# Twelve row buffers in place of eight for the expert gathers of a fused two-block transformer kernel, from set 112 on

## The chip, the cores and the metric

The kernel runs on one core of one Trainium2 chip. The metric is the device time of one execution in microseconds; the time before is the median of three runs. The profiled execution is one more execution, taken by the hardware profiler.

## The reference

Two transformer blocks run one after the other on 256 tokens of width 1024, all in float32. The first block has attention and then a layer with product-key experts; the second has a gated feed-forward network, a mixer, and another feed-forward network. The change touches the expert layer of the first block alone:

```python
def _peer(h, w_query, sub_keys, u, v):
    # 128 tokens at a time: 8 heads, 16 experts for each head, of 128 * 128 experts
    best, flat = lax.top_k(cand, PEER_TOPK)
    ...
    experts = e1 * PEER_N_KEYS + e2
    g = jax.nn.softmax(best, axis=-1)
    u_sel = jnp.take(u, experts, axis=0)
    act = jax.nn.gelu(jnp.einsum('cd,chkd->chk', xc, u_sel).astype(jnp.float32), approximate=False)
    v_sel = jnp.take(v, experts, axis=0)
    return jnp.einsum('chk,chkd->cd', (g * act).astype(v.dtype), v_sel)
```

Every token picks 8 x 16 = 128 experts. For each of them one row of `u` (1024 floats) is fetched for a dot product with the token, and one row of `v` for a weighted sum. That is 256 x 128 x 2 rows of 4 KB, 268 MB, which depend on the data and so must be gathered.

## The kernel before

The tokens stand on the 128 partitions, in two tiles `tt`. A **set** is one gathered piece: for one slot (one of the 128 experts of each token), one row for each of the 128 tokens, 128 x 1024 floats or 512 KB. There are 2 x 128 sets of `u` and as many of `v`, 512 in all, each fetched by one indirect DMA that GpSimd (POOL) issues at L745.

Slots go in groups of eight (`GB`). The list `SETS` sets the order of the gathers: u of group 0, then u of group g and v of group g-1 in turn, and v of the last group at the end. Set n is the n-th gather in this order, so sets 104 to 111 are u of group 7, sets 112 to 119 v of group 6, sets 120 to 127 u of group 8. From set 112 on there are 400 gathers, that is 25 cycles of 16 (eight of v, eight of u).

Set n lands in buffer n % 8. For n below 256 the buffers lie in `ring`, from 256 on in `arena`; it is the same eight semaphore pairs: `rows_ld[i]` counts landings, `rows_used[i]` counts uses. Before POOL issues set n it waits until set n-8 has been used (`used(pool, n - GB)`); POOL issues strictly in the order of n.

The consumers, each in the order of its own program:

- VectorE (DVE) takes every u set with one multiply-and-sum per slot (`dot_rows`, L2026). Behind the first two slots of group g it multiplies the gates of group g-1 (L2033), which ScalarE (ACT) needs for the diagonal matrices (L923).
- TensorE (PE) takes the v sets of the slots with slot % 4 != 3, six of eight (`sum_group`, L1383): a diagonal matrix of gates times the gathered rows, in two halves of 512 columns. Each half is two passes, so a slot has four MATMUL records and a group 24.
- DVE takes the other two v sets of each group (slots 3 and 7) with a multiply-add into `hx` (`add_row`, L2043).
- In some groups DVE also does part of the routing of later slots (`top_keys`, `top_pairs`, `pick`, lines 1931 to 2017), and PE and ACT compute the queries of the second tile.

Behind the last gather SyncE (SP) loads the weights of the first feed-forward network (L621) and PE begins it (L1429) once the sum is added to `hx`. The first two weight pieces are loaded earlier, once set 255 has been used and `ring` is free.

## Time and profile before

| what | value |
|---|---|
| runs (us) | 1599.96, 1591.04, 1595.07; median 1595.07 |
| profiled execution: span from first to last instruction | 1554.8 us |
| median of the runs less that span | 40.3 us |
| PE, DVE, ACT, POOL busy over the span | 79%, 67%, 27%, 37% |
| gathers from set 112 on: first issue to last issue | 384.2 to 946.3 us |

The profile gives the profiled execution's span; a time of its own beside the span isn't recorded. The 40.3 us between the median of the runs and the span stand for what lies around the first and the last instruction, and are the same for every stage. The stretch from 384.1 to 947 us holds the gathers that the change touches, and the 607.8 us behind it hold the second block.

### The profile page before, as it was taken

The page shows a single profiled execution, that of the slowest core. Times are in us where ns is not written, and L with a number is a line of the kernel's source. Part 1 is how long each engine was busy: PE and PEld are TensorE (multiplying, and loading weights), DVE is VectorE, ACT ScalarE, POOL GpSimd, SP SyncE. Part 2 cuts the span into 40 slices and gives each one's busy share as a digit, 9 for nine tenths or more (in the row PEclk, how much of TensorE's full clock was granted, in tenths as well). Part 3 has the DMA queues.
Part 4 walks back from the last instruction along what each step waited for, and adds up shares of the span by engine and source line. Part 5 has one row for each costly group of instructions (what it writes and reads, how often), then busy time and mean ns, then how long its engine had stood idle before and what let it go on. Part 6 is the DMA issues. An engine that isn't in the chain of part 4 may idle for free.

```text
span 1554.8 us, 17801 instructions
## 1 busy us (share of the span) xinstructions
PE 1233.7 (79%) x6525; PEld 893.8 (57%) x6525; DVE 1047.1 (67%) x1923; ACT 426.1 (27%) x738; POOL 572.7 (37%) x626
## 2 busy tenths in 40 slices
PE   6988896667876564575556558999999999999997
PEld 4555574234443221232222225989989999899996
DVE  5767467878588666775665564677776777656556
ACT  1145313021102100200210113333335555344332
POOL 4100016667776666767777774010010000000000
PEclk9996898779888776877787779999999999899999
DMA  9834148999999999999999999678848556355561
GB/s 329 341 121 152 34 178 309 376 363 368 389 396 377 346 379 394 379 362 388 382 368 360 390 358 344 208 269 303 288 150 297 176 168 206 128 162 190 197 207 69
DMA packets 179710, 435.47 MB, mean 280 GB/s; under 512 B 13881, under 2 KB 84610, under 8 KB 179638
## 3 DMA queue, kind: packets, MB, share of 16 engines
q0 software_dynamic: 84384, 306.26, 51.9%
q1 hardware_dynamic: 94214, 126.18, 24.3%
q10 hardware_dynamic: 1040, 2.10, 0.4%
q8 instruction: 41, 0.67, 0.2%
q14 instruction: 31, 0.25, 0.0%
HBM read 433.44 MB, written 2.14 MB: 280 GB/s over the span
## 4 chain that ended last, share of the span: by engine, by line
PE 59%; DMA 14%; POOL 11%; DVE 8%; issue 6%; ACT 2%; SPq 0%; DVEq 0%; POOLq 0%
PE quad L1429 14%; PE quad_a L1383 8%; PE quad L1383 7%; PE quad_a L1534 7%; DMA arena<-in_peer_v_dram,arena 6%; POOL arena L745 6%; PE quad_a L1443 6%; DMA ring<-in_peer_v_dram,arena 5%; POOL ring L745 5%; PE quad_a L1139 3%; PE quad_a L1235 2%; PE quad L1217 2%; PE quad_a L1611 2%; DMA ring<-in_ffn_w_gu_dram 2%; PE quad_a L1599 1%
## 5 line engine op out<-in xcount | busy, mean ns | idle before, releaser
L1383 PE MATMUL quad_a<-arena 128*128 128x512 f32 x384 | 202.2, 691 | 147.6 <-DMA arena<-in_peer_v_dram,arena 147.6
L1383 PE MATMUL quad<-ring,arena 128*128 128x512 f32 x360 | 191.1, 695 | 111.5 <-DMA ring<-in_peer_v_dram,arena 108.1
L1383 PEld LDWEIGHTS quad_a<-arena 128*128 128x128 f32 x384 | 84.6, 225 | 264.6 <-issue 264.3
L745 POOL DMA_INDIRECT ring<-in_peer_u_dram,arena x136 | 137.8, 1013 | 206.2 <-DVE arena L2006 130.8
L1383 PEld LDWEIGHTS quad<-ring,arena 128*128 128x128 f32 x360 | 79.6, 226 | 216.0 <-issue 216.0
L1429 PE MATMUL quad<-u_hi,w_hi 128*128 128x256 f32 x704 | 199.1, 283 | 2.0 <-DVE u_lo L1926 2.0
L1429 PE MATMUL quad<-u_lo,w_hi 128*128 128x256 f32 x704 | 199.1, 283 | 0.0
L1429 PE MATMUL quad<-u_hi,w_lo 128*128 128x256 f32 x704 | 198.9, 283 | 0.0
L1884 DVE TENSOR_TENSOR w_lo<-ring,w_hi 128x2048 fp32r<-128x2048 f32 x66 | 150.7, 2289 | 52.0 <-ACT w_hi L929 51.7
L697 POOL DMA_DIRECT2D arena<-in_w_ada_dram x60 | 31.8, 531 | 400.2 <-DVE arena L1677 395.3
L2026 DVE CUSTOM_DVE_ANT_0 arena<-ring,quad 128x1024 f32<-128x1024 f32 x128 | 154.7, 1220 | 35.3 <-DMA ring<-in_peer_u_dram,arena 19.1
L2026 DVE CUSTOM_DVE_ANT_0 arena<-arena,quad_a 128x1024 f32<-128x1024 f32 x120 | 144.8, 1220 | 23.7 <-DMA arena<-in_peer_u_dram,arena 18.1
L923 ACT ACTIVATE arena<-ident,arena 128x128 f32<-128x128 f32 x192 | 59.6, 389 | 355.7 <-DVE arena L2033 355.7
L745 POOL DMA_INDIRECT arena<-in_peer_u_dram,arena x120 | 130.9, 1091 | 58.7 <-PE quad_a L1383 32.3
L745 POOL DMA_INDIRECT arena<-in_peer_v_dram,arena x136 | 129.7, 954 | 43.1 <-issue 39.4
L929 ACT ACTIVATE w_hi<-ring 128x2048 fp32r<-128x2048 f32 x66 | 126.0, 1914 | 68.6 <-DMA ring<-in_ffn_w_gu_dram 68.6
L1429 PEld LDWEIGHTS quad<-u_hi,w_hi 128*128 128x128 f32 x704 | 134.6, 191 | 4.0 <-issue 1.9
L1429 PEld LDWEIGHTS quad<-u_lo,w_hi 128*128 128x128 f32 x704 | 134.4, 191 | 1.5
L1429 PEld LDWEIGHTS quad<-u_hi,w_lo 128*128 128x128 f32 x704 | 134.4, 191 | 0.0
L745 POOL DMA_INDIRECT ring<-in_peer_v_dram,arena x120 | 113.1, 943 | 40.9 <-issue 36.0
L2043 DVE SCALAR_TENSOR_TENSOR hx<-arena,hx 128x1024 f32<-128x1024 f32 x34 | 43.8, 1289 | 116.8 <-DMA arena<-in_peer_v_dram,arena 116.6
L1534 PE MATMUL quad_a<-u_hi,w_lo 128*128 128x256 f32 x288 | 81.2, 282 | 0.0
(364 smaller groups left out, 2257.2 us busy)
## 6 DMA issues: line engine op xcount, KB each, us to landing
ring<-in_ffn_w_gu_dram SPq DMA_DIRECT2D x44, 1024.0 KB, 9.3
arena<-in_w_ada_dram POOLq DMA_DIRECT2D x60, 512.0 KB, 6.4
ring<-in_ffn_w_down_dram SPq DMA_DIRECT2D x22, 1024.0 KB, 5.0
ring<-in_w_mix_in_dram SPq DMA_DIRECT2D x20, 1024.0 KB, 6.3
arena<-in_peer_w_query_dram SPq DMA_DIRECT2D x4, 2048.0 KB, 7.9
ring<-in_w_ada_dram POOLq DMA_DIRECT2D x12, 512.0 KB, 10.5
arena<-in_w_in_dram SPq DMA_DIRECT2D x3, 2048.0 KB, 35.2
arena<-in_w_out_dram SPq DMA_DIRECT2D x2, 2048.0 KB, 10.8
```

The costliest lines, as they stand in the source:

```text
L697: gp.dma_start(buffer, src).then_inc(ld_ada[i], 16)
L745: gp.indirect_dma_start(out=rows_of(n), out_offset=None, in_=t["peer_" + kind][0], in_offset=bass.IndirectOffsetOnAxis(ap=expert[tt][:, sl ...
L923: diag_ready.mark(ac.activation(diag[:, i % DIAGS], ident, ACT.Copy, scale=gate[tt][:, slot:slot + 1]))
L929: ac.activation(w_hi[slot], w_slots[slot], ACT.Copy).then_inc(hi_ready.sem, 1)
L1139: last = te.matmul(bank[0:ROWS[tt], 0:width], nT[:, k, COL0[tt]:COL0[tt] + ROWS[tt]], rhs[:, k], start=(k == 0), stop=(k == KD - 1))
L1383: last = te.matmul(sum_side[tt][:, cols], diag[:, i % DIAGS], rows_of(n)[:, cols], start=(slot == pe_slots[0]), stop=(slot == pe_slots[-1] ...
L1429: last = te.matmul(psum[c][:, w * SEQ:(w + 1) * SEQ], weight[a][:, k, (c % 2) * P:(c % 2 + 1) * P], (u_hi, u_lo)[b][:, k], start=(k == 0 a ...
L1443: last = te.matmul(psum[4 + 2 * tt + n][:, :], (h_hi, h_lo)[a][:, c, tt * P:(tt + 1) * P], weight[b][:, c % 2, n * 512:(n + 1) * 512], sta ...
L1534: last = te.matmul(bank[:, a * SEQ:(a + 1) * SEQ], w[i][:, k, cols], u[j][:, k], start=start, stop=stop)
L1884: v.tensor_tensor(w_lo[slot], w_slots[slot], w_hi[slot].bitcast(F32), ALU.subtract).then_inc(lo_ready.sem, 1)
L2026: v.tensor_tensor_reduce(out=prod[:, slot % 2], in0=rows_of(n), in1=hn_side[tt], scale=1.0, scalar=0.0, op0=ALU.mult, op1=ALU.add, accum_o ...
L2043: v.scalar_tensor_tensor(out=hx[:, tt], in0=rows_of(n), scalar=gate[tt][:, slot:slot + 1], in1=hx[:, tt], op0=ALU.mult, op1=ALU.add).then_ ...
```

## The change

From set 112 on the gathers rotate over twelve buffers in place of eight. The four more lie in `arena` at columns 0 to 4095 for sets below 256, and at 11776, 12800, 13824 and 14848 from set 256 on. Each set now knows its buffer (`buffer_of`), how many times that buffer has been used (`use_of`), and the set that had it before (`before`). All waits go by these. The first set in a new buffer waits instead for query matmuls of the second tile (`a_full`), which read what lay there. The order of the gathers, all consumers' instructions and their order stay. SP's first weight load waits for the last uses of twelve buffers instead of eight, which are uses of sets up to 255 either way.

```diff
         rows_early = [area(ring, D * i, D) for i in range(GB)]
-        rows_late = [area(arena, o, D) for o in (4096, 5120, 6144, 15872, 16896, 22024, 23048, 24072)]
+        rows_early += [area(arena, D * i, D) for i in range(4)]
+        rows_late = [area(arena, o, D) for o in (4096, 5120, 6144, 15872, 16896, 22024, 23048, 24072, 11776, 12800, 13824, 14848)]
+        BUFFERS, WIDER_AT = len(rows_early), 112
...
+        buffer_of, use_of, before = [], [], []
+        last_in = {}
+        for n in range(2 * QT * SLOTS):
+            i = n % GB if n < WIDER_AT else (n - WIDER_AT) % BUFFERS
+            buffer_of.append(i)
+            before.append(last_in.get(i))
+            use_of.append(1 if before[n] is None else use_of[before[n]] + 1)
+            last_in[i] = n
...
         def used(eng, n):
-            eng.wait_ge(rows_used[n % GB], n // GB + 1)
+            eng.wait_ge(rows_used[buffer_of[n]], use_of[n])
...
-                        for last in range(QT * SLOTS - GB, QT * SLOTS):
+                        for last in range(QT * SLOTS - BUFFERS, QT * SLOTS):
                             used(sp, last)
...
-                    if n >= GB:
-                        used(pool, n - GB)
+                    if before[n] is not None:
+                        used(pool, before[n])
+                    elif n >= WIDER_AT:
+                        pool.wait_ge(a_full.sem, a_at["pq", 1, 0] + 1)
                     elif n == 6:
                         pool.wait_ge(d_full.sem, d_at["wo", 1, 1] + 1)
+                    if n == QT * SLOTS:
+                        pool.wait_ge(a_full.sem, a_at["pq", 1, 3] + 1)
```

On POOL, around the first gather into a new buffer, the program of before reads as follows. The rows are the gathers of sets 118 to 127; `rows_used0` to `rows_used7` are the eight use counts.

```order
L745 DMA ring<-in_peer_v_dram,arena 128x1024 [waits rows_used6]
L745 DMA ring<-in_peer_v_dram,arena 128x1024 [waits rows_used7]
L745 DMA ring<-in_peer_u_dram,arena 128x1024 [waits rows_used0,routed]
L745 DMA ring<-in_peer_u_dram,arena 128x1024 [waits rows_used1]
L745 DMA ring<-in_peer_u_dram,arena 128x1024 [waits rows_used2]
L745 DMA ring<-in_peer_u_dram,arena 128x1024 [waits rows_used3]
L745 DMA ring<-in_peer_u_dram,arena 128x1024 [waits rows_used4]
L745 DMA ring<-in_peer_u_dram,arena 128x1024 [waits rows_used5]
L745 DMA ring<-in_peer_u_dram,arena 128x1024 [waits rows_used6]
L745 DMA ring<-in_peer_u_dram,arena 128x1024 [waits rows_used7]
```

The same place after the change (L760 is the line that was L745), sets 118 to 131:

```order
L760 DMA ring<-in_peer_v_dram,arena 128x1024 [waits rows_used6]
L760 DMA ring<-in_peer_v_dram,arena 128x1024 [waits rows_used7]
L760 DMA arena<-in_peer_u_dram,arena 128x1024 [waits a_full,routed]
L760 DMA arena<-in_peer_u_dram,arena 128x1024 [waits a_full] x3
L760 DMA ring<-in_peer_u_dram,arena 128x1024 [waits rows_used0]
L760 DMA ring<-in_peer_u_dram,arena 128x1024 [waits rows_used1]
L760 DMA ring<-in_peer_u_dram,arena 128x1024 [waits rows_used2]
L760 DMA ring<-in_peer_u_dram,arena 128x1024 [waits rows_used3]
L760 DMA ring<-in_peer_v_dram,arena 128x1024 [waits rows_used4]
L760 DMA ring<-in_peer_v_dram,arena 128x1024 [waits rows_used5]
L760 DMA ring<-in_peer_v_dram,arena 128x1024 [waits rows_used6]
L760 DMA ring<-in_peer_v_dram,arena 128x1024 [waits rows_used7]
```

No gather has moved. The first four of group 8 no longer wait for the v sets just ahead of them, and from there on every wait is for the set twelve earlier instead of eight.

## Rows read from the trace of the kernel before

**Rows 1.** The page: busy tenths, granted clock, DMA share and rate in 40 slices.

```profile
PE   6988896667876564575556558999999999999997
POOL 4100016667776666767777774010010000000000
PEclk9996898779888776877787779999999999899999
DMA  9834148999999999999999999678848556355561
```

**Rows 2.** Windows by stage: stretch and length, busy us of engines, clock, DMA share, GB/s.

```profile
core 0: us, PE busy (x) PEld busy (x) DVE busy (x) ACT busy (x) POOL busy (x), PEclk, DMA share, GB/s
384.10:947.00 562.90, 340.17 (x774) 154.38 (x775) 361.17 (x744) 74.34 (x204) 401.67 (x402) 0.78 0.99 376
947.00:1554.80 607.80, 584.15 (x4267) 549.85 (x4265) 412.82 (x460) 247.54 (x241) 38.08 (x65) 0.98 0.61 206
```

**Rows 3.** Groups of POOL's instructions, 384.1 to 947 us: busy, mean ns, idle before.

```profile
L745 POOL DMA_INDIRECT arena<-in_peer_u_dram,arena x120 | 130.9, 1091 | 58.7 <-PE quad_a L1383 32.3 <-issue 22.9 <-PE quad L1383 2.1
L745 POOL DMA_INDIRECT arena<-in_peer_v_dram,arena x136 | 129.7, 954 | 43.1 <-issue 39.4 <-DVE arena L2026 1.9 <-PE quad_a L1383 1.7
L745 POOL DMA_INDIRECT ring<-in_peer_u_dram,arena x72 | 73.5, 1020 | 37.6 <-PE quad L1383 22.3 <-issue 13.1 <-DVE hx L2043 2.2
L745 POOL DMA_INDIRECT ring<-in_peer_v_dram,arena x72 | 67.4, 937 | 22.0 <-issue 22.0
```

**Rows 4.** Line L745 in that stretch: issue to landing, min/median/max.

```profile
DMA to landing us min/median/max: 4.8/6.2/10.7
```

**Rows 5.** Timeline of POOL, undisturbed stretch: start, us, engine, line, [idle before].

```profile
450.56 0.94 POOL L745 DMA_INDIRECT ring<-in_peer_v_dram,arena  x1 [0.30 <-issue]
...
458.00 0.94 POOL L745 DMA_INDIRECT ring<-in_peer_v_dram,arena  x1 [0.30 <-issue]
```

**Rows 6.** Windows: two undisturbed stretches, one with waits, one with weight loads.

```profile
405.00:415.00 10.00, 5.64 (x24) 3.41 (x23) 6.06 (x10) 1.08 (x4) 7.56 (x9) 0.78 1.03 410
452.00:460.00 8.00, 4.54 (x7) 2.06 (x8) 7.50 (x36) 0.21 (x1) 6.17 (x7) 0.79 1.03 413
...
500.00:516.00 16.00, 11.78 (x24) 4.81 (x23) 14.34 (x35) 1.86 (x6) 9.60 (x10) 0.91 0.91 341
...
606.00:626.00 20.00, 8.88 (x15) 3.88 (x16) 9.87 (x18) 2.07 (x7) 10.89 (x14) 0.66 1.03 400
```

**Rows 7.** Timeline of one v group and the gathers that wait for it.

```profile
865.04 12.01 PE L1383 MATMUL quad_a<-arena 128*128 128x512 f32 x24 [9.65 <-DMA arena<-in_peer_v_dram,arena]
...
868.74 0.94 POOL L745 DMA_INDIRECT arena<-in_peer_u_dram,arena  x1 [0.60 <-PE quad_a L1383]
...
870.46 0.94 POOL L745 DMA_INDIRECT arena<-in_peer_u_dram,arena  x1 [0.77 <-PE quad_a L1383]
872.17 0.94 POOL L745 DMA_INDIRECT arena<-in_peer_u_dram,arena  x1 [0.77 <-PE quad_a L1383]
```

**Rows 8.** Timeline of two DVE multiply-adds and the gathers issued beside them.

```profile
822.36 1.28 DVE L2043 SCALAR_TENSOR_TENSOR hx<-arena,hx 128x1024 f32<-128x1024 f32 x1 [4.04 <-DMA arena<-in_peer_v_dram,arena]
822.49 1.97 POOL L745 DMA_INDIRECT arena<-in_peer_u_dram,arena  x1 [0.48 <-PE quad_a L1383]
...
827.45 1.28 DVE L2043 SCALAR_TENSOR_TENSOR hx<-arena,hx 128x1024 f32<-128x1024 f32 x1 [3.81 <-DMA arena<-in_peer_v_dram,arena]
827.94 1.61 POOL L745 DMA_INDIRECT arena<-in_peer_u_dram,arena  x1 [0.30 <-issue]
```

**Rows 9.** Timeline where routing on DVE delays its two multiply-adds.

```profile
499.72 12.05 PE L1383 MATMUL quad<-ring,arena 128*128 128x512 f32 x24 [8.76 <-DMA ring<-in_peer_v_dram,arena]
...
508.52 2.67 DVE L2043 SCALAR_TENSOR_TENSOR hx<-ring,arena,hx 128x1024 f32<-128x1024 f32 x2
510.07 1.93 POOL L745 DMA_INDIRECT ring<-in_peer_u_dram,arena  x1 [2.23 <-DVE hx L2043]
```

**Rows 10.** Timeline: the two early weight loads, and the longest wait of POOL behind them.

```profile
591.06 1.00 SPq L621 DMA_DIRECT2D ring<-in_ffn_w_gu_dram  x2
...
621.14 0.94 POOL L745 DMA_INDIRECT arena<-in_peer_u_dram,arena  x1 [3.41 <-PE quad_a L1383]
```

**Rows 11.** Timeline: the last gather, and the first matmul of the second block.

```profile
946.34 0.94 POOL L745 DMA_INDIRECT arena<-in_peer_v_dram,arena  x1 [0.30 <-issue]
...
961.80 0.36 PE L1429 MATMUL quad<-u_hi,w_hi 128*128 128x256 f32 x1 [1.13 <-DVE u_lo L1926]
```

More of the change, by code:

```diff
@@ L225, in set_of @@
             return first_set[kind, tt * GROUPS + slot // GB] + slot % GB
+        buffer_of, use_of, before = [], [], []
[6 more added lines that the diff above has]
+            last_in[i] = n
         def rows_of(n):
-            return (rows_early if n < QT * SLOTS else rows_late)[n % GB]
+            return (rows_early if n < QT * SLOTS else rows_late)[buffer_of[n]]
         def on_pe(tt, slot):
@@ L371, in program @@
         bests, softs, routed = signal("bests"), signal("softs"), signal("routed")
-        rows_ld = [sem(f"rows_ld{i}") for i in range(GB)]
-        rows_used = [sem(f"rows_used{i}") for i in range(GB)]
+        rows_ld = [sem(f"rows_ld{i}") for i in range(BUFFERS)]
+        rows_used = [sem(f"rows_used{i}") for i in range(BUFFERS)]
         n_ready = signal("n_ready")
@@ L390, in used @@
         def used(eng, n):
-            eng.wait_ge(rows_used[n % GB], n // GB + 1)
+            eng.wait_ge(rows_used[buffer_of[n]], use_of[n])
         def landed_set(eng, n):
-            eng.wait_ge(rows_ld[n % GB], 16 * (n // GB + 1))
+            eng.wait_ge(rows_ld[buffer_of[n]], 16 * use_of[n])
         PIECES = ((0, 0, 2), (0, 2, 2), (0, 4, 4), (1, 0, 4), (1, 4, 4))
@@ L740, in _ @@
                     n = set_of(kind, tt, slot)
-                    if n >= GB:
-                        used(pool, n - GB)
+                    if before[n] is not None:
+                        used(pool, before[n])
+                    elif n >= WIDER_AT:
+                        pool.wait_ge(a_full.sem, a_at["pq", 1, 0] + 1)
                     elif n == 6:
                         pool.wait_ge(d_full.sem, d_at["wo", 1, 1] + 1)
+                    if n == QT * SLOTS:
+                        pool.wait_ge(a_full.sem, a_at["pq", 1, 3] + 1)
                     gp.indirect_dma_start(out=rows_of(n), out_offset=None, in_=t["peer_" + kind][0],
-                                          in_offset=bass.IndirectOffsetOnAxis(ap=expert[tt][:, slot:slot + 1], axis=0)).then_inc(rows_ld[n % GB], 16)
-            for n in range(len(SETS) * GB - GB, len(SETS) * GB):
+                                          in_offset=bass.IndirectOffsetOnAxis(ap=expert[tt][:, slot:slot + 1], axis=0)).then_inc(rows_ld[buffer_of[n]], 16)
+            for n in range(len(SETS) * GB - BUFFERS, len(SETS) * GB):
                 used(pool, n)
@@ L1384, in sum_group @@
                                          stop=(slot == pe_slots[-1]), skip_group_check=True)
-                    last.then_inc(rows_used[n % GB], 1)
+                    last.then_inc(rows_used[buffer_of[n]], 1)
             pe.wait_ge(d_free.sem, len(d_jobs))
@@ L2026, in dot_rows @@
                     v.tensor_tensor_reduce(out=prod[:, slot % 2], in0=rows_of(n), in1=hn_side[tt], scale=1.0, scalar=0.0, op0=ALU.mult,
-                                           op1=ALU.add, accum_out=dots[tt][:, slot:slot + 1]).then_inc(rows_used[n % GB], 1)
+                                           op1=ALU.add, accum_out=dots[tt][:, slot:slot + 1]).then_inc(rows_used[buffer_of[n]], 1)
             def gate_group(group):
@@ L2043, in add_row @@
                 v.scalar_tensor_tensor(out=hx[:, tt], in0=rows_of(n), scalar=gate[tt][:, slot:slot + 1], in1=hx[:, tt],
-                                       op0=ALU.mult, op1=ALU.add).then_inc(rows_used[n % GB], 1)
+                                       op0=ALU.mult, op1=ALU.add).then_inc(rows_used[buffer_of[n]], 1)
             def add_sum(tt):
```

## The prediction

> **What bounds the kernel now.** I read the page's forty slices first [rows 1]: between slice 8 and slice 24 POOL is busy six to seven tenths, PE five to eight, and the DMA engines nine or more. This is the gather stage. Behind it PE is at nine tenths and the DMA drops to about half. So the program has two parts with different limits, and the change can move only the first. The windows give the sizes [rows 2]: 562.9 us from the first gather that the change touches to just behind the last, and 607.8 us for the second block, which follows the last gather by a fixed chain: last issue 946.34, first matmul of the feed-forward network 961.80 [rows 11]. Whatever the 400 gathers save comes off the end one to one, unless the second block changes its own pace.
>
> Second, what sets the pace of the gathers. The groups of POOL's instructions [rows 3] divide the stretch completely: busy 130.9 + 129.7 + 73.5 + 67.4 = 401.5 us, idle 58.7 + 43.1 + 37.6 + 22.0 = 161.4 us, together 562.9 us, that is 1.407 us a gather. An undisturbed gather takes POOL 0.94 us and stands 0.30 us behind the one before [rows 5]; six steps from 450.56 to 458.00 give 7.44 / 6 = 1.24 us. For 400 gathers that is 376 us busy and 120 us idle, 496 us. What is left has two causes:
> - idle 161.4 - 120 = **41.4 us**, waits for a buffer's last use. Nearly all of it stands ahead of u sets and is ended by PE at L1383, the rest by DVE at L2043 and L2026 [rows 3].
> - busy 401.5 - 376 = **25.5 us**, gathers that take longer than 0.94 us.
>
> Third, why POOL waits for PE. One cycle shows it [rows 7]: the first v set has landed at 865.04 and PE starts; the three gathers at 868.74, 870.46 and 872.17 wait 0.60, 0.77 and 0.77 us for its slots 0, 1 and 2. A landing takes a median of 6.2 us [rows 4], and the first slot is given back about 3.4 us after PE starts (868.74 less POOL's 0.30), so a buffer is tied up 6.2 + 3.4 + 0.3 = 9.9 us. Eight buffers at 1.24 us are 9.92 us: there is no slack at all, and each disturbance is a wait. Once DVE was late with routing, its multiply-adds began at 508.52 and POOL waited 2.23 us [rows 9].
>
> Fourth, whether the DMA engines could go faster, since their share is 0.99 [rows 2]. Share is not rate. In stretches without waits they move 410 and 413 GB/s, in one with waits 341 [rows 6], and the mean is 376 [rows 2]. A set is 128 x 4096 bytes = 524,288 bytes, so 410 GB/s is 1.28 us a set against 1.407 now. The floor of the DMA is thus 400 x 1.28 = 512 us, plus the two weight pieces of 1 MB issued at 591.06 [rows 10], 2.1 MB / 410 GB/s = 5.1 us: 517 us.
>
> The Trainium skill speaks against this room: "DMA: Bandwidth & Descriptors", section "Bandwidth", says that for HBM to SBUF the limit is about 358 GB/s a core, with the fabric's 435 behind it. By the first figure a set would be 1.46 us and 400 of them 586 us, more than the stretch takes now, and no buffer would help; by the second 1.205 us. The trace disagrees with the first (376 mean, 413 undisturbed, with one core running) and lies under the second.
>
> **The change part by part.**
> - *Reuse distance 8 to 12 for sets from 120 on.* A buffer may now be tied up for 12 x 1.24 = 14.9 us. The ordinary loop needs 9.9 us, which leaves 5 us. The worst consumer: PE's group began at 499.72 with the landing of slot 0, slot 3 landed some 3 x 1.28 = 3.8 us later, at 503.5, and its multiply-add ended at 508.52 + 1.3 = 509.8, 6.3 us later [rows 9]; 6.2 + 6.3 + 0.3 = 12.8 us still fits. So I take the 41.4 us as gone. Bounds: 0 us left; or, if long landings (10.7 us at most [rows 4]) and late consumers meet often, a quarter left, 10 us.
> - *Weight loads at 591.06.* With both in flight landings stretch, and POOL's longest wait, 3.41 us, is paid behind them [rows 10], while the rate there stays at 400 GB/s [rows 6]. That wait is thus mostly a backlog in the DMA queues and not lost rate. With twelve buffers the backlog stays in the queues. The 5.1 us of DMA work remain.
> - *The long gathers, 25.5 us.* Beside the multiply-adds of DVE a gather takes 1.97 us if it starts 0.13 us behind the DVE instruction's start, and 1.61 us if 0.49 us behind: it ends 2.1 us after that start both times [rows 8]. In-between starts follow from that; 50 multiply-adds lie in the 25 cycles, so 25.5 us is 0.51 us for each. A gather stream without waits starts once every 1.24 us, so one start falls into each 1.28 us of DVE work, at any phase; delays of 0 to 1.03 us have a mean near 0.5. I keep 25.5 us. Bounds: 0 (phases that never meet) and 50 x 1.03 = 51.5 us.
> - *First use of the new buffers.* Four gathers from set 120 wait for a query product that PE finishes behind group 5, whose v sets are 96 to 103, more than sixteen gathers earlier; set 256 waits for one behind group 9. Both are done long before; cost nothing, and if not, once, under 3 us. The `routed` wait of set 120 is unchanged and DVE had sent it before.
> - *SP's wait for twelve last uses* ends with the same set 255, and *POOL's wait ahead of the second block's loads* with the same set 511: nothing. Counting and address changes cost no instruction.
>
> **Sum.** POOL then needs 496 + 25.5 = 521.5 us for the stretch, the DMA 517. The two bounds are 4.5 us apart, and each must now and then wait for the other: POOL's delay of 1 us empties a short queue, which is not made up at 1.28 against 1.24. I add 2.5 us: **524 us**, 39 us less than 563. The profiled span would be 1554.8 - 39 = 1516; the median of the runs 1595.07 - 39 = **1556 us**. PE and DVE do not stand in the way: 340 and 361 us busy in the stretch [rows 2], 65% and 69% of 524 us.
>
> The skill has a rule on the long gathers. "SBUF — State Buffer", section "SBUF: two separate sides", says that while DVE runs a two-port instruction GpSimd is locked out and cannot write the descriptors of its DMAs. The rows have the effect, yet only for starts inside the DVE instruction. By the rule taken in full, all of 50 x 1.28 = 64 us would be lost, and the stretch would be 560 us.
>
> **The rivals.**
> - *Locks take the place of waits.* Today three gathers of each cycle wait for PE, and where they then start is set by PE. Freed, POOL's phase against DVE's multiply-adds is set by the landing time; if it settles at the bad phase, each costs 1.03 us: 496 + 51.5 = 547.5 us, a saving of 15, **1580 us**. For it: 822.49 and 827.94 are both hit in one cycle [rows 8]. Against it: a delay shifts the phase, and two hits of 1.03 us a cycle exceed what the DMA backlog can keep steady. If the whole 1.28 us counts each time, as the rule has it, it is 560 us and 1592 us. Chance 0.08.
> - *The DMA engines are the limit already.* Share 0.99 [rows 2] speaks for it; the rates of [rows 6] against it. It would give nothing: **1594 us**. Chance 0.05.
> - *Late consumers still stall POOL* (a quarter to a half of the 41.4 us remains): 1566 to **1577 us**. The 12.8 us above is close to 14.9, and routing ends soon after the middle of the stretch. Chance 0.10.
> - *Slower: more sets in flight slow each other.* With up to twelve open in place of eight, memory or queues could serve them at a worse pace than 1.28 us. It decides above 1.407 us a set; at 1.45 us the stretch is 580 us and the time **1612 us**. For it: behind the loads at 591.06 landings took up to 10.7 us [rows 4, 10]. Against it: in just that stretch, with the most in flight, the DMA moved 400 GB/s [rows 6], 1.31 us a set. Chance 0.03.
>
> **How the numbers follow.** Forecast 0.74, rivals 0.08, 0.05, 0.10, 0.03. The forecast's own range is 517 to 531 us for the stretch, 1549 to 1563; noise of the runs is 4 us either way. To hold 8 in 10 I take in the late consumers and part of the locks: 1546 to 1574. A change of 0.5%, 8 us, is about what this measurement can tell. Faster than 1587: forecast, late consumers and nearly all of the locks, 0.91; within 8 us: 0.06; slower: 0.03.
>
> **What would show it.** Right: from set 112 on POOL's idle falls to about 120 us, with next to nothing ended by PE; 1.30 to 1.31 us a gather; over 400 GB/s throughout; the second block still 608 us. The long gathers tell the locks: POOL busy near 401 us if I am right, near 427 in the rival. Wrong: idle time under PE or DVE that stays; a GB/s that doesn't rise with POOL unblocked; or a second block that grows by what the first gives back.

## The result, and the profile after

The change made the kernel faster by about half a per cent: 1588.23 us against 1598.01 us for the kernel before, the medians of 20 runs each, ratio 0.9946 with a 95% interval of 0.9931 to 0.996. The medians differ by 9.8 us, where 39 were forecast. The profiled execution of the changed kernel took 1585.36 us, with a span of 1583.6 us.

One thing has to be said ahead of every other number. The program runs at one of two levels, and in every session that follows all executions of a kernel are at the same one. Each session ran on another chip, so chip and session can't be told apart. In three sessions (chips 2, 3 and 8) the kernel before took 1555 to 1561 us, in three others (chips 4, 14 and 12) and in the recorded comparison 1591 to 1598 us. I call them the **quick** and the **dragging** sessions. All kernels named together below ran in one session. One case doesn't fit unless its profile came from another session or chip, which isn't on record: the profile of before has a span of 1554.8 us, while its 20 timed runs took 1591 to 1604.

The page of the changed kernel in its recorded, dragging session, in the same 40 slices as [rows 1]:

```profile
PE   6987996558767547556644666999999999999997
POOL 4100034666666767666677666110001000000000
PEclk9987898788888677778777768999999999999999
DMA  9843157989999889999999999687759456446561
```

The DMA engines now fall to eight tenths in several slices of the gather stage, where [rows 1] had nine throughout. That is the opposite of what the forecast asked for. The windows by stage answer to [rows 2]; the stretches begin at the first gather that the change touches (397.8 us) and behind the last (issued at 975.1 us):

```profile
core 0: us, PE busy (x) PEld busy (x) DVE busy (x) ACT busy (x) POOL busy (x), PEclk, DMA share, GB/s
397.70:976.00 578.30, 345.93 (x774) 157.18 (x775) 357.14 (x745) 73.70 (x203) 396.91 (x402) 0.78 0.96 366
976.00:1583.60 607.60, 583.17 (x4268) 548.09 (x4266) 412.87 (x460) 248.98 (x243) 37.92 (x65) 0.99 0.60 206
```

The second block is what it was, 607.6 us against 607.8. The gather stretch is *longer* than in the profile before, 578.3 against 562.9 us, and the DMA moves 366 GB/s in place of 376. Also the 396 us ahead of the change's first gather, which the change does not touch, are 13.6 us longer (397.8 against 384.2). So this profile and the one before are not of the same level, and their difference is not the change's effect.

The groups of POOL's instructions in that stretch, in place of [rows 3]:

```profile
L760 POOL DMA_INDIRECT arena<-in_peer_v_dram,arena x160 | 152.0, 950 | 71.1 <-issue 45.6 <-remote 25.2 <-DVE arena L2041 0.3
L760 POOL DMA_INDIRECT arena<-in_peer_u_dram,arena x144 | 149.9, 1041 | 60.3 <-issue 44.8 <-remote 11.0 <-DVE hx L2058 4.6
L760 POOL DMA_INDIRECT ring<-in_peer_u_dram,arena x48 | 49.3, 1027 | 29.9 <-issue 13.7 <-DVE hx L2058 12.6 <-remote 3.5
L760 POOL DMA_INDIRECT ring<-in_peer_v_dram,arena x48 | 45.3, 944 | 20.2 <-issue 13.4 <-remote 6.5 <-DVE arena L2041 0.3
```

Busy time sums to 396.5 us. Idle time sums to 181.5 us, of which 117.5 stand under "issue" and some 64 are waits. The waits thus did not vanish. They stand ahead of v sets as well as u sets, and most are ended by "remote": the profile has the semaphore update that ended the wait, but no instruction that ended just before that update.

### The profile page after: what moved, and what is told of

Same layout as the page of the kernel before. It is cut to its first block, busy times and chain, and to the rows that moved or that the text cites. A ratio compares the mean times of both kernels' runs of the same rounds, so it can differ in the third digit from the quotient of the medians.

```text
span 1583.6 us, 17806 instructions
## 1 busy us (share of the span) xinstructions
PE 1240.4 (78%) x6525; PEld 895.3 (57%) x6525; DVE 1042.5 (66%) x1923; ACT 426.1 (27%) x738; POOL 570.2 (36%) x626
## 4 chain that ended last, share of the span: by engine, by line
PE 46%; POOL 21%; issue 10%; DVE 10%; DMA 6%; another core or an unknown queue 5%; ACT 2%; SPq 0%; DVEq 0%; POOLq 0%
POOL arena L760 16%; PE quad L1444 14%; PE quad_a L1549 7%; PE quad_a L1458 6%; POOL ring L760 5%; PE quad_a L1154 3%; DMA ring<-in_peer_u_dram,arena 2%; PE quad_a L1250 2%; PE quad L1232 2%; DMA ring<-in_ffn_w_gu_dram 2%; PE quad_a L1626 2%; PE quad_a L1398 1%; PE quad_a L1614 1%; PE quad_a L1472 1%
## 5 line engine op out<-in xcount | busy, mean ns | idle before, releaser
L1398 PE MATMUL quad<-ring,arena 128*128 128x512 f32 x288 | 152.5, 689 | 92.4 <-DMA ring<-in_peer_v_dram,arena 79.7
L760 POOL DMA_INDIRECT ring<-in_peer_u_dram,arena x112 | 115.3, 1030 | 203.4 <-DVE arena L2021 129.2
L760 POOL DMA_INDIRECT arena<-in_peer_v_dram,arena x160 | 152.0, 950 | 71.1 <-issue 45.6
L760 POOL DMA_INDIRECT arena<-in_peer_u_dram,arena x144 | 149.9, 1041 | 60.3 <-issue 44.8
L1398 PEld LDWEIGHTS quad<-ring,arena 128*128 128x128 f32 x288 | 62.9, 224 | 175.9 <-issue 175.9
L2041 DVE CUSTOM_DVE_ANT_0 arena<-arena,quad_a 128x1024 f32<-128x1024 f32 x124 | 148.5, 1219 | 6.6 <-DMA arena<-in_peer_u_dram,arena 3.6
L2041 DVE CUSTOM_DVE_ANT_0 arena<-ring,quad 128x1024 f32<-128x1024 f32 x108 | 128.7, 1219 | 27.6 <-DMA ring<-in_peer_u_dram,arena 16.6
L2058 DVE SCALAR_TENSOR_TENSOR hx<-arena,hx 128x1024 f32<-128x1024 f32 x40 | 51.4, 1284 | 142.5 <-DMA arena<-in_peer_v_dram,arena 126.6
L760 POOL DMA_INDIRECT ring<-in_peer_v_dram,arena x96 | 90.7, 945 | 46.5 <-issue 27.5
L1398 PE MATMUL quad<-arena 128*128 128x512 f32 x96 | 54.4, 727 | 40.8 <-DMA arena<-in_peer_v_dram,arena 40.8
```

What stands on the lines that cost most here:

```text
L760: gp.indirect_dma_start(out=rows_of(n), out_offset=None, in_=t["peer_" + kind][0], in_offset=bass.IndirectOffsetOnAxis(ap=expert[tt][:, sl ...
L1398: last = te.matmul(sum_side[tt][:, cols], diag[:, i % DIAGS], rows_of(n)[:, cols], start=(slot == pe_slots[0]), stop=(slot == pe_slots[-1] ...
L2041: v.tensor_tensor_reduce(out=prod[:, slot % 2], in0=rows_of(n), in1=hn_side[tt], scale=1.0, scalar=0.0, op0=ALU.mult, op1=ALU.add, accum_o ...
L2058: v.scalar_tensor_tensor(out=hx[:, tt], in0=rows_of(n), scalar=gate[tt][:, slot:slot + 1], in1=hx[:, tt], op0=ALU.mult, op1=ALU.add).then_ ...
```

## The experiments

**Session on chip 2: each kernel once.** Was the difference between the two profiles the change's? `b0_before` is the kernel before, `a0_after` the changed one, both as they are.

> The kernel before, unchanged, profiled again. The profile of before that the forecast rests on has a span of 1554.8 us, while its timed runs have a median of 1598 us; the changed kernel's profiled run (span 1583.6) agrees with its timed runs. Theory A (the profile of before was an unusually undisturbed execution): this profile has a span near 1590 to 1600 us, and from set 112 on POOL's idle time beyond 0.30 us a gather is 70 us or more in place of 41, with waits of 2 to 4 us that no consumer in the records explains. Theory B (the program's other stages differ): the gathers from set 112 on take 563 us again and the 40 us lie elsewhere.

> The changed kernel, unchanged, profiled again on the same chip. Theory A: span 1580 to 1590 us, the stretch from set 112 on 575 to 580 us, POOL idle beyond 0.30 us a gather about 60 us, most of it in waits of 2 to 6 us about every 16 gathers, and hardly any of the 0.8 us waits for PE. Theory B: the stretch is near the forecast 524 us.

Measured: before 1555.71 us (another run 1560.86), span 1554.0, gathers of sets 112 to 511 from 380.1 to 945.4 us, that is 565.3 us from the first issue to the last. After 1514.77 us, span 1513.1, the same gathers from 380.5 to 901.3, 520.8 us. This is close to the forecast's stretch (524 us) and its gain (39 us; here 40.9 between the two profiled executions), so the second of the two theories, B, holds on chip 2. It also shows that a profiled execution's time is only 1.7 us above its span, and not 40.

**Session on chip 4: how many buffers, and where.** `a1_after` is the changed kernel; `e10_ten_buffers` has ten buffers in place of twelve; `e256_second_half` has eight until set 255 and twelve behind.

```diff
# e10_ten_buffers
-        rows_early += [area(arena, D * i, D) for i in range(4)]
+        rows_early += [area(arena, D * i, D) for i in range(2)]
-        rows_late = [... 24072, 11776, 12800, 13824, 14848)]
+        rows_late = [... 24072, 11776, 12800)]
# e256_second_half
-        BUFFERS, WIDER_AT = len(rows_early), 112
+        BUFFERS, WIDER_AT = len(rows_early), 256
```

> The changed kernel, unchanged, timed. On the chip of the first two looks it was 41 to 46 us under the kernel before (1514.8 against 1555.7 and 1560.9), where the twenty recorded runs had 10 us between the medians (1588.2 against 1598.0). Theory C (the conditions of the execution differ, and the change is worth about 40 us in undisturbed ones and 10 in disturbed ones): wherever the kernel before takes 1556 to 1561 us, this one takes 1515 to 1520, ratio 0.973; where it takes about 1598, this one takes about 1588, ratio 0.994. Theory D (the recorded comparison was of unlike conditions, and the change is worth 40 us everywhere): ratio 0.973 whatever the kernel before takes.

> Ten buffers in place of twelve from set 112 on; the outputs are the same. If the gain is the slack in the loop of issue, landing and release (9.9 us against eight buffers' 9.92), ten buffers (12.4 us) hold the ordinary loop and lose only the cycles in which routing on VectorE or the early weight loads stretch it (12.8 us and more): 33 to 38 us of the 41 are gained. If the number of buffers counts for itself (a deeper DMA queue moves data faster), the gain is about half, 20 us.

> Twelve buffers from set 256 on alone (WIDER_AT 256), eight before; the outputs are the same. Between the two looks the sets 112 to 255 took 201.7 and 186.8 us, the rest 363.6 and 334.0. So this kernel should gain 27 to 30 us where the changed one gains 41 to 45, and its gathers 112 to 255 should keep the waits of 0.8 us for PE.

| kernel | us, median | ratio to before (1590.78) | 95% | sets 112 to 511, us |
|---|---|---|---|---|
| a1_after | 1582.86 | 0.9957 | 0.9937 to 0.9976 | 569.8 |
| e10_ten_buffers | 1583.95 | 0.9962 | 0.9943 to 0.9982 | 579.0 |
| e256_second_half | 1581.54 | 0.9953 | 0.9932 to 0.9974 | 573.8 |

A dragging session. The gain is the small one that theory C has for such a session; the 33 to 38 us expected of ten buffers and the 27 to 30 of the second half did not come. The three can't be told apart by their times, and the extent of the stretch varies between executions by as much as between them (after: 569.8 to 577.3 in four profiles). One comparison inside the traces, of one execution each: sets 120 to 256 went at 1.457 us a gather with eight buffers (e256) and at 1.458 with twelve (a1). There the four added buffers bought nothing.

**Session on chip 3: sixteen buffers.** `b2_before_timed` and `a2_after_look` are the two kernels; `e16_sixteen_late` has eight buffers until set 255 and sixteen behind, four of them in `ring`.

```diff
-        rows_early += [area(arena, D * i, D) for i in range(4)]
-        rows_late = [area(arena, o, D) for o in (4096, 5120, 6144, 15872, 16896, ...)]
-        BUFFERS, WIDER_AT = len(rows_early), 112
+        rows_early += [area(arena, D * i, D) for i in range(4)] * 2
+        rows_late = [area(arena, o, D) for o in (4096, 5120, 6144, 15872)] + [area(ring, 4096 + D * i, D) for i in range(4)]
+        rows_late += [area(arena, o, D) for o in (16896, 22024, 23048, 24072, 11776, 12800, 13824, 14848)]
+        BUFFERS, WIDER_AT = len(rows_early), 256
...
+                        for last in range(len(SETS) * GB - 12, len(SETS) * GB - 8):
+                            used(sp, last)
```

> The kernel before, unchanged, timed and profiled in the same way as the changed one was (11 runs or so). In the profiles of the three timed kernels so far semaphore updates are missing (8,600 to 9,400 of 14,290) and POOL waits 2 to 4 us at a time for releases of PE that the matmul records place 6 us earlier; in the two looks nothing is missing and no such wait occurs. Theory C (these late releases are part of the execution): the span is about 1590 us, its gathers from set 112 on take about 590 us, and waits for PE have grown beyond 0.8 us. Theory D (they came with the change): span near 1556 us and complete records.

> The changed kernel, unchanged, one look on the same chip as the timed runs beside it. If the chip makes the difference: near 1583 us here. If it is the way of running (one look against repeated timed runs): near 1515 us again, with complete records.

> Sixteen buffers from set 256 on (four more in ring columns 4096 to 8191, with a wait of the third weight load for their last uses), eight before; the outputs are the same. Against the kernel with twelve from 256 on (ratio 0.9953 when timed). Theory E (late releases of PE, about 18 us from issue to reuse, set the pace when timed): sixteen buffers cover 19.8 us, so the waits mostly go, 10 to 15 us more gained, ratio 0.986 to 0.989. Theory F (something else stops POOL, whatever the buffers): no further gain, ratio 0.995.

Measured: before 1556.03 us against 1557.01 for its own second copy (ratio 0.9999, 0.9969 to 1.0029), stretch 562.6 us; after, one run, 1519.51 us, stretch 520.7; sixteen late 1533.27 us (four runs), 0.9843 (0.9775 to 0.9911), stretch 533.0. A quick session. From set 256 on sixteen buffers took 331.5 us and twelve 334.0 (336.6 in the quick session on chip 8): beyond twelve there is hardly anything to have, as the loop's arithmetic said. Theories E and F were about dragging sessions and stay untested here. Over the whole stretch this kernel is 12.3 us behind twelve buffers: 14.8 lost on sets 112 to 255 with its eight early buffers, 2.5 won behind.

**Session on chip 14: is it PE?** `b3_before` and `a3_after` are the two kernels. `p8_half_pe` (eight buffers) and `p12_half_pe` (twelve) leave out PE's second 512 columns of the v sets, except at the first and last slot that PE has in a tile of 128 slots, so that PE gives buffers back sooner.

```diff
-                    for half in range(2):
+                    for half in range(2 if slot in (pe_slots[0], pe_slots[-1]) else 1):
```

> The kernel before, unchanged, with the changed one and two variants on one chip. So far two kinds of sessions: in one the kernel before takes 1556 us and the changed one 1515 to 1520, all records complete; in the other 1591 to 1598 and 1583 to 1588, with semaphore updates missing. This run says which kind the session is, and gives the profile of before in it. In a session of the second kind: gathers from set 112 on about 590 us, with waits for PE that are longer than 0.8 us.

> The changed kernel, unchanged. In a session of the first kind a timed ratio of 0.974 (0.971 to 0.978), which would say that the sum of the forecast was right for it; in one of the second kind 0.994 to 0.996.

> Eight buffers; PE multiplies only the first 512 of 1024 columns of each v set except the first and last slot of a tile, so the sum over experts is wrong in the other half, and PE has half the instructions in a v group (12 in place of 24). PE then gives a buffer back 1.7 us after landing in place of 3.4, and the loop is 8.2 us against 9.92. Theory of the tight loop: most of POOL's 41 us of waits go without any more buffers, ratio 0.978 to 0.985 in a session of the first kind (the waits for VectorE stay). If instead releases of PE are late because PE's signals or records back up (the second kind of session), half the instructions also cure much of that: ratio 0.96 to 0.97 there. If the waits were for something else than PE's release, ratio 1.00.

> Twelve buffers with the same half of PE's work left out. Theory of the tight loop: nothing is left for it to cure, so it is within 3 us of the changed kernel in a session of the first kind (ratio to before 0.974), at most 0.5% better. In a session of the second kind: if backed-up signals of PE set the pace, it comes near 1520 us (ratio 0.955) where the changed kernel has 1585; if it stays at 1585, PE's signals aren't the cause.

| kernel | us, median | ratio to before (1590.81) | 95% | sets 112 to 511, us |
|---|---|---|---|---|
| b3_before | 1593.74 | 1.0011 | 0.9982 to 1.004 | 592.4 |
| a3_after | 1578.1 | 0.9919 | 0.989 to 0.9948 | 574.5 |
| p8_half_pe | 1601.56 | 1.0067 | 1.0038 to 1.0095 | 585.6 |
| p12_half_pe | 1590.68 | 0.9987 | 0.9961 to 1.0013 | 574.4 |

A dragging session, and the first in which the kernel before itself has a profile. Its groups and its window, against [rows 2, 3]:

```profile
L745 POOL DMA_INDIRECT arena<-in_peer_u_dram,arena x120 | 134.0, 1117 | 68.1 <-issue 33.7 <-PE quad_a L1383 15.1 <-DVE hx L2043 11.0
L745 POOL DMA_INDIRECT arena<-in_peer_v_dram,arena x136 | 130.2, 957 | 42.8 <-issue 42.0 <-PE quad_a L1383 0.8
L745 POOL DMA_INDIRECT ring<-in_peer_u_dram,arena x72 | 74.5, 1035 | 54.0 <-issue 22.7 <-PE quad L1383 20.4 <-DVE hx L2043 8.0
L745 POOL DMA_INDIRECT ring<-in_peer_v_dram,arena x72 | 67.5, 938 | 22.0 <-issue 22.0
```

```profile
396.20:989.70 593.50, 340.30 (x775) 154.75 (x776) 361.46 (x744) 74.24 (x204) 406.69 (x402) 0.78 0.94 357
```

Busy 406.2 us, near the 401.5 of before; idle 186.9 against 161.4. The 593.5 us are 30.6 more than the 562.9 of [rows 2], with the same work on PE (340 us) and DVE (361 us) and at the same granted clock. Between the first gather (215.3 us, in before 217.2) and set 112 another 12 us went (396.3 against 384.2), and behind the last issue none (1597.6 - 988.7 = 608.9 us; in [rows 2, 11] 1554.8 - 946.3 = 608.5). So what a dragging session adds lies in the gather stage alone. A piece of its timeline shows what it looks like. PE works on the queries of the second tile; the rows are in order of their start:

```profile
418.84 0.27 PE L1235 MATMUL quad_a<-arena 128*128 128x128 f32 x1 [0.42 <-issue]
...
420.94 0.27 PE L1235 MATMUL quad_a<-arena 128*128 128x128 f32 x1 [1.83 <-issue]
...
422.36 0.27 PE L1235 MATMUL quad_a<-arena 128*128 128x128 f32 x1 [1.14 <-issue]
...
424.46 0.37 PE L1235 MATMUL quad_a<-arena 128*128 128x128 f32 x1 [1.84 <-issue]
...
434.85 0.94 POOL L745 DMA_INDIRECT ring<-in_peer_u_dram,arena  x1 [7.16 <-PE quad L1383]
```

Matmuls of 0.27 to 0.37 us follow one another with 1.1 to 1.8 us between them, "<-issue": PE waits for nothing that the profile shows, and in the program these matmuls (`query_columns`) have no wait between them. The DMAs that load instructions took no longer than in `b0_before` (0.3 to 0.4 us for 8 KB and 0.9 to 1.1 us for 16 KB in both, between 380 and 620 us). Missing matmul records are not the reason: the pages of before, b3 and all others with PE's full work count the same 6525 instructions of PE. PE's group of v sets starts late behind this, and POOL waits 7.16 us for it. The DMA is not slow meanwhile, as the window over those ten microseconds shows:

```profile
420.00:430.00 10.00, 1.66 (x5) 1.52 (x6) 4.49 (x7) 0.60 (x2) 5.85 (x7) 0.64 1.02 406
```

It moves 406 GB/s, near the 410 of [rows 6]. In the gather stage of the quick profiles there is no such gap of 0.35 to 3.5 us under "issue" on PE, in those of the dragging ones 5 to 27. And less PE work helped little. In the stretch, twelve buffers take 574.4 us with half of PE's columns and 574.5 with all; eight take 585.6 against 592.4. Over the whole program both are slower than their counterparts (p8 by 7.8 us beside b3, p12 by 12.6 beside a3), and the profiles put that ahead of set 112, which is issued at 405.4 us against 396.3, and at 403.7 against 395.5 (from 215 to 396 us the granted clock was 0.75 in both against 0.82 and 0.84). The granted clock over the span fell from 0.873 (b3) to 0.831 (p8) and from 0.878 (a3) to 0.835 (p12). So half of PE's instructions in the v groups did not cure the dragging: p12 did not come near 1520 us. That does not clear PE's signals, as the traces read below show.

**Session on chip 12: sixteen buffers again, and thin consumers.** `a4_after` and `e16b_sixteen_late` are as above. `t8_thin` (eight buffers) and `t12_thin` (twelve) leave out most of the consumers' work on the gathered rows: PE multiplies 64 of each 512 columns, except at its first and last slot of a tile, and DVE's dot products and multiply-adds take 64 of 1024 columns. The gathers stay whole.

```diff
-                        cols = slice(512 * half, 512 * half + 512)
+                        cols = slice(512 * half, 512 * half + (512 if slot in (pe_slots[0], pe_slots[-1]) else 64))
...
-                    v.tensor_tensor_reduce(out=prod[:, slot % 2], in0=rows_of(n), in1=hn_side[tt], ...
+                    v.tensor_tensor_reduce(out=prod[:, slot % 2, 0:64], in0=rows_of(n)[:, 0:64], in1=hn_side[tt][:, 0:64], ...
...
-                v.scalar_tensor_tensor(out=hx[:, tt], in0=rows_of(n), ...
+                v.scalar_tensor_tensor(out=hx[:, tt, 0:64], in0=rows_of(n)[:, 0:64], ...
```

> The changed kernel, unchanged. In a session of the first kind (kernel before at about 1556 us) the timed ratio that is still missing: 0.974, between 0.971 and 0.978. In one of the second kind (before at 1591 or more) again 0.992 to 0.996.

> Sixteen buffers from set 256 on, eight before, once more: in the first kind of session it had ratio 0.9843. In the second kind, where twelve buffers still wait with 17 to 20 us from issue to reuse: if these late releases can be covered, sixteen buffers (19.8 us) remove most of the waits behind set 256, 20 of 35 us, ratio 0.984 to 0.988; if each stall ends in a wait however many buffers there are, the ratio is that of twelve from 256 on, 0.995.

> Eight buffers with thin consumers: all gathers, waits and signals are there, but PE multiplies 64 columns per half (except the first and last slot of a tile), and DVE's dot products and multiply-adds take 64 of the 1024 columns, so the expert layer's output is wrong. The loop is 6.2 + 0.5 + 0.3 = 7 us and nothing locks POOL for long. First kind of session: gathers at the DMA's 1.28 us from set 112 on, 515 to 520 us for the stretch, waits near 0. Second kind: if the length of the consumers' work matters, the same 1.28; if signals between the engines are what is late there, the stretch stays at 560 us or more although there is hardly any work.

> Twelve buffers with the same thin consumers. First kind: within 2 us of the eight-buffer one, since the loop has slack already and the DMA's pace is all that is left. Second kind: tells whether buffers help against late signals when the work is gone; if it takes 20 us less than the eight-buffer one, they do, if the same, they don't.

| kernel | us, median | ratio to before (1595.69) | 95% | sets 112 to 511, us |
|---|---|---|---|---|
| a4_after | 1588.88 | 0.9961 | 0.9936 to 0.9986 | 575.4 |
| e16b_sixteen_late | 1594.05 | 0.999 | 0.997 to 1.0011 | 580.5 |
| t8_thin | 1584.63 | 0.9917 | 0.9881 to 0.9953 | 578.5 |
| t12_thin | 1574.89 | 0.9863 | 0.982 to 0.9906 | 567.0 |

A dragging session; `t12_thin` has two timed runs. From set 256 on sixteen buffers took 367.9 us and twelve (a4) 365.8, so there was no further gain, as theory F had it. More buffers did not end POOL's waits; the time from issue to reuse grew instead. The second row here is one of POOL's waits in `e16b_sixteen_late`: the set that was in its buffer had been issued 25.3 us earlier, where sixteen undisturbed gathers take 16 x 1.24 = 19.8 us:

```profile
L763 POOL DMA_INDIRECT ring<-in_peer_v_dram,arena x64 | 63.8, 996 | 37.4 <-issue 19.6 <-remote 17.8
...
643.81 1.94 POOL L763 DMA_INDIRECT arena<-in_peer_v_dram,arena  x1 [5.08 <-DVE hx L2061]
```

With thin consumers DVE is busy for 117 us of the stretch in place of 361, PE for 198 in place of 340, and eight buffers still take 578.5 us. That is above the 560 us which the expectation had for late signals between the engines; twelve buffers take 11.5 us less, between its two cases:

```profile
393.60:973.20 579.60, 198.23 (x781) 169.50 (x781) 117.13 (x745) 73.99 (x204) 379.69 (x402) 0.53 0.97 366
```

**Session on chip 8: the quick counterpart.** `a5_after` is the changed kernel, `t8b_thin` is `t8_thin`.

> The changed kernel, unchanged, in the hope of a session of the first kind: there a timed ratio of 0.974 (0.971 to 0.978). In one of the second kind 0.992 to 0.996 for the sixth time, and nothing new.

> Eight buffers and thin consumers (PE 64 of 512 columns per half, DVE 64 of 1024, output wrong) once more, as the control for the second kind of session, where its stretch from set 112 on took 578.5 us with all semaphore waits at work and hardly any arithmetic. In a session of the first kind it should run at the DMA's pace, 515 to 520 us; if it takes 560 us or more there too, the tight loop theory is wrong also where the forecast came true. In the second kind: 575 to 585 us again.

Measured, a quick session with before at 1557.10 us: after **1517.21 us, ratio 0.9756 (0.9735 to 0.9777)**, stretch 522.6 us; t8b_thin 1506.55 us, 0.9683 (0.965 to 0.9717, two runs), stretch 520.0 us. The thin window beside the one just shown is the same instructions and clock, 58.5 us shorter, and at 405 in place of 366 GB/s:

```profile
370.80:891.90 521.10, 198.41 (x772) 170.02 (x772) 117.75 (x744) 73.21 (x204) 382.19 (x402) 0.53 1.02 405
```

The difference is again waits of POOL, 86 us in `t8_thin` against 33, and 68 of the 86 are ended by "remote". The first row is of `t8_thin`, the second of `t8b_thin`:

```profile
L745 POOL DMA_INDIRECT arena<-in_peer_u_dram,arena x120 | 114.4, 953 | 83.3 <-remote 36.6 <-issue 32.7 <-DVE hx L2043 9.9
```

```profile
L745 POOL DMA_INDIRECT arena<-in_peer_u_dram,arena x120 | 117.1, 976 | 46.1 <-issue 30.2 <-PE quad_a L1383 8.7 <-PE quad L1383 6.3
```

The changed kernel in the quick session, windows and POOL groups, against [rows 2, 3]:

```profile
381.90:905.00 523.10, 339.13 (x769) 153.23 (x770) 359.36 (x744) 73.77 (x204) 396.39 (x402) 0.81 1.02 404
905.00:1511.30 606.30, 583.27 (x4272) 547.82 (x4270) 412.77 (x460) 247.75 (x242) 38.41 (x65) 0.99 0.62 207
```

```profile
L760 POOL DMA_INDIRECT arena<-in_peer_v_dram,arena x160 | 152.2, 951 | 48.7 <-issue 48.3 <-PE quad_a L1398 0.4
L760 POOL DMA_INDIRECT arena<-in_peer_u_dram,arena x144 | 148.6, 1032 | 48.8 <-issue 42.0 <-PE quad_a L1398 4.5 <-DVE hx L2058 2.3
L760 POOL DMA_INDIRECT ring<-in_peer_u_dram,arena x48 | 50.6, 1055 | 14.6 <-issue 14.6
L760 POOL DMA_INDIRECT ring<-in_peer_v_dram,arena x48 | 45.0, 937 | 14.6 <-issue 14.6
```

Idle is 126.7 us, of which 119.5 are "issue"; waits are 7.2 us in place of 41.4. One v group of it, where [rows 7] had three waits:

```profile
874.85 0.94 POOL L760 DMA_INDIRECT arena<-in_peer_u_dram,arena  x1 [0.30 <-issue]
875.31 1.28 DVE L2058 SCALAR_TENSOR_TENSOR hx<-arena,hx 128x1024 f32<-128x1024 f32 x1 [3.89 <-DMA arena<-in_peer_v_dram,arena]
876.10 1.32 POOL L760 DMA_INDIRECT arena<-in_peer_u_dram,arena  x1 [0.30 <-issue]
877.72 0.94 POOL L760 DMA_INDIRECT arena<-in_peer_u_dram,arena  x1 [0.30 <-issue]
```

PE had begun this group at 871.59. The waits have gone; the gather of 876.10, begun 0.79 us into the multiply-add, takes 1.32 us and ends 2.1 us after that instruction's start, by the same pattern as [rows 8]. The price of more sets in flight shows in the landings, against [rows 4]:

```profile
DMA to landing us min/median/max: 5.9/7.4/13.6
```

## Why the prediction was wrong

**The step that failed** is the last of the sum: "the profiled span would be 1554.8 - 39 = 1516; the median of the runs 1595.07 - 39 = 1556 us". It took the 40.3 us between span and median for time around the first and last instruction. The runs with both numbers have 1.7 to 1.8 us there (1513.06 against 1511.3; 1585.36 against 1583.6; 1599.35 against 1597.6). So the profile of before was of a quick execution, and the three timed runs of dragging ones, whose extra time of about 40 us lies in the gather stage (b3: 12 ahead of set 112, 30 behind). The misplaced 40 us alone would leave the forecast of the median where it is. What moves it is what they stood for: the 39 us were worked out on a quick execution and taken off a dragging one, in which the change gives 9.8. The forecast's argument was about an execution that the measured runs were not. Worked out for the recorded profile: 53.3 us more in the stretch than forecast (577.3 against 524), 13.6 ahead of it, none behind it; less the 38.5 us that I had set outside the span and that aren't there; plus 2.9 from this one execution to the median. Together 31.3 us, where the median is 32.2 above the forecast.

**What held, in the quick sessions:**
- *Stretch 524 us.* Measured 520.8, 520.7 and 522.6. *Gain 39 us.* Measured 1557.10 - 1517.21 = 39.9 us.
- *The 41.4 us of waits go.* 7.2 us stayed, most behind the early weight loads (POOL waits 1.85, 1.21 and 0.77 us for PE at 605.80, 607.95 and 609.67 in a5), where the forecast said the backlog would stay in the queues. My bounds were 0 and 10.
- *The long gathers stay.* POOL busy 396.4 us, 20.4 over 376, where I had 25.5. With multiply-adds of 64 columns the four groups are busy for 381.7 us (t8b), 14.7 less: most of the excess is theirs. The rival of locks, near 427, is out. So is the rule of the Trainium skill, "SBUF — State Buffer", section "SBUF: two separate sides", if the whole DVE instruction is counted as lock-out: the stretch would have been 560 us.
- *Floor of the DMA 517 us.* Eight buffers with thin consumers came to 520.0 at 405 GB/s. This is the nearest that any kernel came, and twelve buffers with full consumers are within 3 us of it. The rival "the DMA engines are the limit already" is out for the quick sessions. The figure of about 358 GB/s in the Trainium skill, "DMA: Bandwidth & Descriptors", section "Bandwidth", is passed by 404 over 523 us. The same section gives it also as a core's share when both cores of a memory domain stream; here one core runs.
- *The second block's 608 us* held within 2 us in two profiles (606.3 in a5, 607.6 in the recorded one). In two others it grew: behind the last issue a0 has 611.8 us and a2 613.4, against 608.5 before, so 3 to 5 us of the gain were given back there.

**What did not hold, in the dragging sessions.** "A buffer may now be tied up for 14.9 us, the ordinary loop needs 9.9" rests on a loop whose parts are fixed times: landing, consumer, signal. If only that loop had been longer by a fixed time, more buffers would have covered it. Ten, twelve and sixteen did not: 579.0, 569.8 to 577.3, and 580.5 us (sixteen from set 256 on), against 592.4 with eight, where the quick sessions have 521 to 523 with twelve. The pace stays at 1.43 to 1.46 us a gather for all of them. At a fixed pace the time from issue to reuse must grow with the count; in the wait shown it was 25.3 us with sixteen. Nor did taking work from the consumers bring the pace of the quick sessions (p12 574.4, t8 578.5, t12 567.0). So the slack of the twelve buffers takes off only a part: 7 to 13 us by the four differences of medians (18 in the stretch by the one pair of profiles, 592.4 to 574.5); the rest is a limit that buffers don't touch. By its time the result, 1588.2, lies among the rivals of locks (1580, or 1592 if the whole instruction counts) and of the DMA's limit (1594), by its signs at neither: POOL's busy time is 396.9 and not 427, and the DMA moved 366 GB/s, less than the 376 of the profile before. The rival of late consumers is near in kind, waits that outlast the buffers, but it priced them by PE and DVE as they run in the quick profile.

What POOL waits for there can be read from the recorded profile of the changed kernel. The gather at 420.79 is set 128, whose buffer holds set 116, slot 4 of a v group. The last of PE's four matmuls on that set ended at 413.75. Its semaphore update is recorded at 420.53, and the two engines that need it, ACT for a diagonal matrix and POOL for the buffer, both start right behind. ACT's copy at 422.90 waits for the matmuls of L1272, which ended at 418.07:

```profile
417.02 1.05 PE L1272 MATMUL quad_a<-arena 128*128 128x128 f32 x8
...
420.56 0.40 ACT L938 ACTIVATE arena<-ident,arena 128x128 f32<-128x128 f32 x1 [1.68 <-remote]
420.79 0.94 POOL L760 DMA_INDIRECT ring<-in_peer_v_dram,arena  x1 [2.79 <-remote]
...
422.90 0.60 ACT L788 ACTIVATE arena<-quad_a 128x512 f32<-128x512 f32 x1 [1.94 <-remote]
```

In this profile 22 gathers from set 112 on stand more than 0.4 us behind the one before. Of them 18 start 1.4 to 9.6 us, in the median 7.3, behind the recorded end of the last instruction on the set that they replace, always one of PE's; 47.7 us of POOL's idle time stand ahead of these 18. The other three dragging profiles of the changed kernel have 16 or 17 such gathers, with medians of 7.4 to 7.6 us. In a5 there are four waits, and each ends 0.27 us behind the last user. So in the dragging executions the releases of PE reach POOL late by PE's own records, also with half of PE's columns (p12: 9 of 15 waits) and with thin consumers (t8: 31 of 37). The data are not late: from issue to the last packet of a set's rows it is 5.6 us in the median in the recorded profile and 5.5 in a5.

**What stays open** is why PE's releases come late, in which chips or sessions, and whether PE's signals are held back or its matmuls really end later than they are recorded. As the whole cause the runs exclude the count of buffers, the columns that PE and DVE work through, and a lower rate of the DMA in itself (406 GB/s while PE stood still). The clock was no lower: 0.78 in the stretch before, in b3 and in the recorded profile. Two more things go with the dragging sessions in every profile: gaps on PE between instructions that wait for nothing shown, and missing records. The quick traces hold 14,286 to 14,290 semaphore updates and 11,651 landings each; the dragging ones 8,000 to 10,000 and 5,800 to 7,800, and those missing all lie in the gather stage. Lost records alone are not the matter, since POOL and ACT did start late. That the recording itself holds the engines up is a rival that no run excludes: a span and a granted clock are on record for every timed run, so none ran unrecorded. Against it as the only cause stands that the quick executions were recorded as well, with all their updates. No kernel here thins out the signals, and the same kernel was not timed twice on one chip on different occasions.

## What to carry to other kernels

Before a span is used to forecast a timed median, set the profiled execution's own time beside the timed runs: 40 us of 1595 that stand "outside" the profile are more likely 40 us of a stage that it did not show. Buffers tied up for a fixed time are counted by latency over cadence (here 9.9 / 1.24 = 8 for no slack at all, 12 for 5 us of it), and once the DMA's floor is near, more give nothing: sixteen bought 2.5 us over twelve. If the pace stays the same as buffers are added, their number isn't the limit; then compare the end of each buffer's last use with the start of the gather that replaces it. Here that shows releases of PE some 7 us late, and the next kernel to try, untested, is one in which PE sends fewer signals, not one with more buffers.

## What the runs showed of the hardware that I had not expected

- The same program has two levels, by session or chip, 1555 to 1561 and 1591 to 1598 us, and nearly all of the difference lies in the stage of the 512 gathers. The changed kernel gains 2.4% at one level and 0.4 to 0.8% at the other.
- Less work on TensorE was no gain, even a loss: with half of the v columns left out on PE the time rose by 0.5 to 0.8%, while the granted clock over the span went from 0.873 to 0.831. How much of the loss is the clock's was not measured by itself, nor was this kernel run in a quick session.
- Most slow gathers start inside a multiply-add of DVE, 33 of the 37 over 1.05 us in the profile of before and 39 of 45 in a5, and all but one of them end about 2.1 us after that instruction's start, whether they started 0.13, 0.49 [rows 8] or 0.79 us into it. The others start inside a TENSOR_TENSOR of DVE (the gather at 807.62 in the profile of before takes 1.90 us beside that of L1884).
- In the dragging executions semaphore updates of PE are recorded up to several us behind the matmul that sends them (420.53 against 413.75 in the recorded profile), in the quick ones 0.01 us behind it in the median.
- With one core running, gathers of 4 KB rows held 404 GB/s over 523 us.
